# The index key projected ahead of the value tiles, with its narrow columns copied aside

## The chip, the cores and the metric

The kernel runs on one core of a Trainium2 chip, in float32 throughout. The metric is the device time of one execution in microseconds (us); lower is better. Times are medians over several executions, and a profile is of one execution.

## The reference, cut to what matters

The program is two transformer-like blocks over 256 tokens of width 1024. The change lies in the first block, where one normalised and modulated activation `hn` (256 x 1024) is projected by one wide matrix, whose columns are then split:

```
hn   = modulate(rmsnorm(x, norm1_g), shift1, scale1)
proj = hn @ w_in                       # 1024 columns in, 11 groups of columns out
qa, ka, va, qi, ki, wi, qb, kb, vb, ga, gb = split(proj)
score = sum_h relu(qi_h @ ki^T) * wi_h * scale     # index scores choose 64 keys per query
ya = attention over the chosen keys (qa, ka, va, rel_bias)
yb = stick-breaking attention (qb, kb, vb)
mod = silu(c) @ w_ada + b_ada          # six modulation vectors of 1024, used all through the block
```

Three of these groups matter here: the values `va` and `vb` (1024 columns together), the index key `ki` (64 columns) and the index weights `wi` (8 columns, one per index head). The last part of `mod` is computed beside them.

## The kernel before, in words

The kernel is written for the five engines by hand. It is a row of blocks; in each block every engine has its own program, the engines meet through semaphores, and at the end of a block all of them drain and are released together before the next begins.

The activation lies transposed in `k.h` (128 partitions x 8 slices x tokens). Weights stream from HBM through a ring of eight half slots (`k.ring`), four chunks of 1 MB at a time. The order of all chunks is a list made once by `plan()` (line 99), and SyncE issues them in that order: `refill()` (line 185) issues the next load as soon as the chunk that held its place is used up, after waiting for a count of finished tiles that the caller names. `arrived()` (line 201) makes an engine wait for a chunk's landing, `chunk()` (line 208) names its place in the ring.

`opening_inputs()` (line 321) computes the first projections, with tokens along the free axis. `block1_projections()` (line 493) is the stage that the change rewrites:

- TensorE (line 505) computes eight value tiles: four chunks `c` of 256 columns, and for each the two halves `tt` of the tokens, eight products each, into bank `2 * c + tt`. From the fifth chunk it then takes the narrow products of `wi` (8 columns, two halves of tokens x 8 slices, line 517) into bank 1, after VectorE has emptied that bank, and last the index key (line 522) into bank 0, after ScalarE has emptied that. In the program that is 64, 16 and 8 products; the trace shows each of them as two passes, 128, 32 and 16.
- ScalarE (line 527) copies the even banks to `v` and last the index key to `kit` (line 533).
- VectorE (line 536) copies the odd banks to `v` (line 539). Behind each of its four copies stand four or five calls of `ada_column()` (line 294): one column of the modulation each, a product of 1024 elements and a sum (line 305), 18 in this block (4, 5, 4 and 5). After the last it scales the narrow sums into `wi` (line 545) and finishes the modulation (lines 312 and 548).
- GpSimd (line 552) moves the bias rows through HBM and loads further modulation weights, each after a count of finished columns (line 290).

`block1_attention()` (line 572) follows: the index scores on TensorE (line 613), ScalarE (line 711) and VectorE (lines 741, 743), and then sixteen items of attention, with sixteen wide gate tiles (line 639) on TensorE between them. Behind it lie `merge1`, `project_and_square` and the expert layer.

VectorE's and TensorE's order around the end of the stage is set by these lines:

```
for c in range(4):                     # VectorE
    dve.wait_ge(k.tile_ready.sem, k.tile_ready.at(2 * c + 2))
    nc.vector.tensor_copy(v[:, 1, ...], k.bank[2 * c + 1][:, 0:256]).then_inc(k.dve_emptied.sem, 1)
    for j in ...: ada_column(k, dve, j)
```

Of the kernel before, what the change touches and what calls it, by code (L numbers as in the profile page):

```python
# [18 lines left out]
ALU = mybir.AluOpType  # L19
ACT = mybir.ActivationFunctionType  # L20
AX = mybir.AxisListType

P = 128
D = 1024
KD = D // P
TOK = 256
TT = TOK // P
# [5 lines left out]
IDX_SCALE = 64 ** -0.5 * 8 ** -0.5  # L33
# [65 lines left out]
def plan():  # L99

    global NDENSE
    unit = 0
    for name, chunks in (("in1", 10), ("v1", 4), ("ki", 1), ("in1g", 8), ("projab", 4), ("out1", 4), ("wq1", 8), ("keys1", 1), ("wq1", 8), ("keys1", 1),
                         ("uv1", 0), ("in2", 14), ("in2g", 4), ("glu", 1), ("ssmout", 2), ("mlout", 4), ("out2", 4),
                         ("wq2", 8), ("keys2", 1), ("wq2", 8), ("keys2", 1), ("uv2", 0)):
        PHASE[name] = len(LOADS)
        if chunks:
            at = DENSE_AT.setdefault(name, NDENSE)
            for c in range(chunks):
                LOADS.append(("dense", at + c, unit, 2))  # L110
                unit += 2
            NDENSE = max(NDENSE, at + chunks)
            continue
        order = [("u", e) for e in range(NKEYS) if e not in AHEAD_UPS] + [("v", e) for e in range(NKEYS)]
        for side, e in order:
            LOADS.append((side + name[-1], e, unit, 1))
            unit += 1
# [67 lines left out]
def refill(k, sp, n, used, counts, after=None):  # L185


    for c in range(n):
        if after is not None:
            after(c)  # L190
        gone = k.at + c
        for m in range(k.loaded, NLOADS):
            if FREED_BY[m] > gone:
                break
            sig, count = counts[c] if used is None else (used, counts[c])
            sp.wait_ge(sig.sem, sig.at(count))
            load(k, sp, m)
            k.loaded = m + 1


def arrived(k, eng, c):

    n = k.at + c
    slot = LOADS[n][2] % HALVES
    eng.wait_ge(k.w_loaded[slot], ARRIVED[n])


def chunk(k, c):

    _, _, unit, size = LOADS[k.at + c]  # L210
    slot = unit % HALVES
    return k.ring[:, slot:slot + size, :].rearrange("p a n -> p (a n)")
# [96 lines left out]
def ada_finish(k, dve, ch, j0, j1):  # L309

    dve.wait_ge(k.ada_done.sem, k.ada_done.at(j1))
    ch.then(k.nc.vector.tensor_tensor(k.mod[:, j0:j1], k.mod[:, j0:j1], k.vec("b_ada")[:, j0:j1], ALU.add))
# [177 lines left out]
    k.trans_ready.advance(HEADS)  # L490


def block1_projections(k, pt, v, kit, wi, row, bias1):


    nc = k.nc
    with nc.Block() as block:
        @block.sync
        def _(sp):
            refill(k, sp, 5, k.tile_ready, [2, 4, 6, 8, 10])  # L500

        @block.tensor
        def _(pe):
            for c in range(4):
                arrived(k, pe, c)
                w = chunk(k, c).rearrange("p (k n) -> p k n", k=KD)
                for tt in range(TT):
                    for kk in range(KD):
                        ins = nc.tensor.matmul(k.bank[2 * c + tt][:, 0:256], k.h[:, kk, tt * P:(tt + 1) * P], w[:, kk, :],
                                               start=kk == 0, stop=kk == KD - 1)  # L510
                    ins.then_inc(k.tile_ready.sem, 1)
            arrived(k, pe, 4)
            w = chunk(k, 4).rearrange("p (k n) -> p k n", k=KD)
            pe.wait_ge(k.dve_emptied.sem, k.dve_emptied.at(1))
            for tt in range(TT):
                for kk in range(KD):
                    ins = nc.tensor.matmul(k.bank[1][:, tt * 8:tt * 8 + 8], k.h[:, kk, tt * P:(tt + 1) * P],
                                           w[:, kk, P:P + 8], start=kk == 0, stop=kk == KD - 1)
            ins.then_inc(k.tile_ready.sem, 1)
            pe.wait_ge(k.act_emptied.sem, k.act_emptied.at(1))  # L520
            for kk in range(KD):
                ins = nc.tensor.matmul(k.bank[0][:, 0:TOK], w[:, kk, 0:P], k.h[:, kk, 0:TOK],
                                       start=kk == 0, stop=kk == KD - 1)
            ins.then_inc(k.tile_ready.sem, 1)

        @block.scalar
        def _(act):
            for c in range(4):
                act.wait_ge(k.tile_ready.sem, k.tile_ready.at(2 * c + 1))
                nc.scalar.activation(v[:, 0, c * 256:(c + 1) * 256], k.bank[2 * c][:, 0:256], ACT.Copy)\  # L530
                    .then_inc(k.act_emptied.sem, 1)
            act.wait_ge(k.tile_ready.sem, k.tile_ready.at(10))
            nc.scalar.activation(kit[:, :], k.bank[0][:, 0:TOK], ACT.Copy)

        @block.vector
        def _(dve):
            for c in range(4):
                dve.wait_ge(k.tile_ready.sem, k.tile_ready.at(2 * c + 2))
                nc.vector.tensor_copy(v[:, 1, c * 256:(c + 1) * 256], k.bank[2 * c + 1][:, 0:256])\
                    .then_inc(k.dve_emptied.sem, 1)  # L540
                left = ADA_TILES - ADA_IN1
                for j in range(ADA_IN1 + left * c // 4, ADA_IN1 + left * (c + 1) // 4):
                    ada_column(k, dve, j)
            dve.wait_ge(k.tile_ready.sem, k.tile_ready.at(9))
            nc.vector.tensor_scalar(wi[:, :], k.bank[1][:, 0:16], IDX_SCALE, None, ALU.mult)
            ch = Chain(dve, k.dve_step)
            ada_finish(k, dve, ch, ADA_FIRST, ADA_TILES)
            ch.then(nc.vector.scalar_tensor_tensor(k.gain[:, 1, :], k.mod[:, 4 * KD:5 * KD], 1.0, k.vec("norm2_g"),
                                                   ALU.add, ALU.mult))

        @block.gpsimd
        def _(pool):
            def modulation_weights(c):
                pool.wait_ge(k.ada_done.sem, k.ada_done.at(2 * (c - ADA_SLOTS) + 2))
                ada_load(k, pool, c)

            pool.wait_ge(k.bias_rows.sem, k.bias_rows.at(HEADS))
            pool.dma_start(k.bias_dram, row).then_inc(k.bias_dma, 16)
            for c in range(ADA_CALLED, ADA_CALLED + 2):
                modulation_weights(c)  # L560
            pool.wait_ge(k.bias_dma, 16)
            src = bass.AP(k.bias_dram.tensor, P - 1, [[HEADS * 3 * P - 1, P], [3 * P, HEADS], [1, 2 * P]])
            pool.dma_start(bias1[:, :, :], src).then_inc(k.bias_dma, 16)
            for c in range(ADA_CALLED + 2, ADA_TILES // 2):
                modulation_weights(c)
    k.tile_ready.advance(10)
    k.act_emptied.advance(4)
    k.dve_emptied.advance(4)
    k.at += 5


# [1825 lines left out]
def build(nc, args, out, stop=None):  # L2397

    k = K()
# [6 lines left out]
    with ExitStack() as ctx:  # L2406
# [31 lines left out]
        def done(what):  # L2438
            return stop == what
# [16 lines left out]
        with ExitStack() as ctx1:  # L2456
            sb1 = lambda n, s: ctx1.enter_context(nc.sbuf_tensor(n, s, F32))
            pt = sb1("proj_t", [P, 36, TOK])
            v = sb1("values", [P, TT, D])
            kit = sb1("ki_t", [P, TOK])  # L2460
            wi = sb1("wi", [P, 16])
            bias0 = sb1("bias0", [P, HEADS, P])
            bias1 = sb1("bias1", [P, HEADS, 2 * P])
            with ExitStack() as ctx2:
                k.ada = ctx2.enter_context(nc.sbuf_tensor("ada", [P, ADA_SLOTS, 2, D], F32))
                k.cond = ctx2.enter_context(nc.sbuf_tensor("cond", [P, D], F32))
                row = pt[:, 20:32, :].rearrange("p a n -> p (a n)").rearrange("p (h n) -> p h n", h=HEADS)
                opening_inputs(k, vecs, row, bias0[0:BUCKETS, :, :], pt)
                block1_projections(k, pt, v, kit, wi, row, bias1)
            yt = sb1("y_t", [P, KD, TOK])  # L2470
            merged = sb1("merged", [P, KD, TOK])
            block1_attention(k, pt, v, kit, wi, bias0, bias1, yt)
            if done("att"):
                return finish(yt[:, :, :])
            merge1(k, pt, yt, merged)
            project_and_square(k, merged, k.mod[:, 2 * KD:3 * KD], yt, k.choice[:, 0, :])
# [7 lines left out]
        with ExitStack() as ctx1:  # L2484
            sb1 = lambda n, s: ctx1.enter_context(nc.sbuf_tensor(n, s, F32))
# [144 lines left out]
```

## Time and profile before

| | before |
|---|---|
| median of 3 runs | 1990.54 us (1987.36 to 1993.57) |
| profiled execution | 1990.65 us |
| its span in the trace | 1988.8 us |
| TensorE busy | 1923.3 us (97%) |
| VectorE busy | 1265.2 us (64%) |
| ScalarE busy | 471.3 us (24%) |
| GpSimd busy | 349.6 us (18%) |
| mean granted TensorE clock | 0.994 |

The span is the time from the first to the last instruction on the core; 1.85 us of the execution lie around it. Times in the trace count from the span's start. TensorE's busy time is modelled, since its products are pipelined, so 97% does not say that it works at its peak. The granted clock is 1.00 at 2.4 GHz and 0.50 at 1.2 GHz. In the rows, PE is TensorE's products, PEld its weight loads, DVE is VectorE, ACT ScalarE, POOL GpSimd and SP SyncE; a name with q is the engine's sequencer.

### The profile page before, as it was taken

Reading aid. Unit: us, or ns where it says so; the run is one execution under the profiler, and the core shown is the slowest. Engines: PE = TensorE matmul, PEld = TensorE weight load, DVE = VectorE, ACT = ScalarE, POOL = GpSimd, SP = SyncE. Lnnn points to the kernel's source line nnn. Section 1 sums busy time; section 2 is a strip of 40 time slices with the busy share of each in tenths; the row PEclk is TensorE's granted clock in tenths of the full one; section 3 lists DMA queues with packets and bytes.
Section 4 is the critical chain, followed back from the end, with each engine's and each line's share of the span. In section 5 each row is a group of like instructions: output and inputs, shape, how many; then the busy total and the mean of one; then the engine's idle time right before and its main releaser. Section 6 shows DMA issues by size and latency. Waiting matters only on the chain. (4 is left out here: it accounts for less than half of the span.)

```text
span 1988.8 us, 33132 instructions
## 1 busy us (share of the span) xinstructions
PE 1923.3 (97%) x13047; PEld 1803.6 (91%) x13047; DVE 1265.2 (64%) x2827; ACT 471.3 (24%) x1646; POOL 349.6 (18%) x304
## 2 busy tenths in 40 slices
PE   8989999999999999999999989999999999999998
PEld 6877789999999999999988567899999999999998
DVE  6349323899788854444489984219997888544343
ACT  3003302223544410000221024012125444100001
POOL 0100000022332312211000740000223323211110
PEclk9989999999999999999999999999999999999999
DMA  8962238799999999999544130378899999999995
GB/s 308 421 260 100 86 148 346 267 372 331 382 398 390 394 416 413 414 414 413 210 141 157 46 114 1 117 282 323 342 334 370 399 381 398 413 413 414 414 414 213
DMA packets 123356, 604.94 MB, mean 304 GB/s; under 512 B 14589, under 2 KB 16797, under 8 KB 83137
## 3 DMA queue, kind: packets, MB, share of 16 engines
q1 hardware_dynamic: 90832, 379.62, 49.5%
q0 software_dynamic: 30800, 222.07, 27.9%
q8 instruction: 104, 1.70, 0.3%
q10 hardware_dynamic: 1568, 1.12, 0.2%
q14 instruction: 52, 0.42, 0.1%
HBM read 600.14 MB, written 2.62 MB: 303 GB/s over the span
## 5 line engine op out<-in xcount | busy, mean ns | idle before, releaser
L1156 PE MATMUL bank<-expert_coef,ring 128*128 128x160 f32 x4096 | 561.4, 299 | 6.1 <-DVE expert_coef L1490 2.9
L1156 PEld LDWEIGHTS bank<-expert_coef,ring 128*128 128x128 f32 x4096 | 557.0, 190 | 9.8 <-DMA ring<-in_uv 6.2
L1131 PE MATMUL bank<-h,ring 128*128 128x160 f32 x3712 | 521.7, 299 | 0.0
L1131 PEld LDWEIGHTS bank<-h,ring 128*128 128x128 f32 x3712 | 508.1, 190 | 0.0
L1082 POOL DMA_INDIRECT expert_rows<-in_uv,pair_index x192 | 274.3, 1428 | 1273.4 <-DVE pair_sum L1374 504.6
L1367 DVE CUSTOM_DVE_ANT_0 expert_rows<-expert_rows,h_tokens 128x1024 f32<-128x1024 f32 x192 | 234.7, 1222 | 230.9 <-DMA expert_rows<-in_uv,pair_index 230.8
L1374 DVE SCALAR_TENSOR_TENSOR pair_sum<-expert_rows,pair_coef,pair_sum 128x1024 f32<-128x1024 f32 x192 | 246.3, 1283 | 57.2 <-ACT pair_coef L1270 55.7
L1268 ACT ACTIVATE pair_act<-pair_dot 128x1 f32<-128x1 f32 x192 | 38.8, 202 | 520.6 <-DVE pair_dot L1367 520.3
L1097 PE MATMUL bank<-h,ring 128*128 128x128 f32 x1024 | 115.7, 276 | 1.1 <-ACT h L1277 1.1
L1097 PEld LDWEIGHTS bank<-h,ring 128*128 128x128 f32 x1024 | 115.4, 192 | 1.3 <-issue 1.2
L1246 ACT ACTIVATE expert_coef<-bank 128x160 f32<-128x160 f32 (+28 forms) x254 | 65.7, 261 | 157.0 <-PE bank L1131 157.0
L1254 ACT ACTIVATE work<-work,choice 128x128 f32<-128x128 f32 x320 | 102.0, 406 | 0.0
L1481 DVE TENSOR_TENSOR work<-const,choice 128x1024 f32<-128x1024 f32 x80 | 97.4, 1222 | 0.4 <-DVE picked L1473 0.4
L1148 PE MATMUL bank<-work 128*128 128x128 f32 x640 | 84.8, 275 | 5.5 <-ACT work L1254 5.5
L1148 PEld LDWEIGHTS bank<-work 128*128 128x128 f32 x640 | 79.3, 191 | 6.4 <-ACT work L1254 6.4
L1244 ACT ACTIVATE expert_act<-bank 128x4 f32<-128x4 f32 (+24 forms) x150 | 35.9, 239 | 165.9 <-PE bank L1131 164.2
L1490 DVE TENSOR_TENSOR expert_coef<-bank,expert_coef 128x212 f32<-128x212 f32 (+19 forms) x80 | 42.4, 530 | 48.1 <-ACT expert_coef L1262 48.1
L1660 PE MATMUL bank<-h,ring 128*128 128x272 f32 (+1 forms) x320 | 71.9, 387 | 1.0 <-PEq L1056 1.0
L1660 PEld LDWEIGHTS bank<-h,ring 128*128 128x128 f32 x320 | 60.7, 190 | 12.1 <-issue 1.4
L398 PE MATMUL bank<-h,ring 128*128 128x256 f32 x320 | 70.3, 380 | 0.0
L398 PEld LDWEIGHTS bank<-h,ring 128*128 128x128 f32 x320 | 60.4, 190 | 10.2 <-issue 2.2
L1941 POOL TENSOR_TENSOR mixed<-s_z,s_rot 128x256 f32<-128x256 f32 x64 | 49.0, 786 | 100.0 <-DVE s_z L1915 100.0
(389 smaller groups left out, 2040.3 us busy)
## 6 DMA issues: line engine op xcount, KB each, us to landing
ring<-in_uv SPq DMA_DIRECT2D x256, 512.0 KB, 13.5
ring<-in_ut SPq DMA_DIRECT2D x232, 512.0 KB, 7.3
ring<-in_dense SPq DMA_DIRECT2D x96, 1024.0 KB, 5.0
ada<-in_ada POOLq DMA_DIRECT2D x16, 1024.0 KB, 17.6
expert_coef<-in_ut SPq DMA_DIRECT2D x24, 512.0 KB, 9.2
ada<-in_ada SPq DMA_DIRECT2D x8, 1024.0 KB, 24.0
expert_rows<-in_uv,pair_index POOLq DMA_INDIRECT x192, 9.4
bias_rows<-proj_t POOLq DMA_DIRECT2D x1, 1536.0 KB, 6.5
```

What stands on the lines that cost most here:

```text
L398: return nc.tensor.matmul(k.bank[j % BANKS][:, 0:TOK], w[:, kk, (j % 2) * P:(j % 2 + 1) * P], k.h[:, kk, 0:TOK], start=kk == 0, stop=kk == ...
L1082: pool.indirect_dma_start(rows[:, p % BUFFERS, :], None, table, bass.IndirectOffsetOnAxis(pindex[:, p:p + 1], 0))\
L1097: ins = nc.tensor.matmul(k.bank[c % 4][:, 0:P], w[:, kk, (c % 2) * P:(c % 2 + 1) * P], k.h[:, kk, tt * P:(tt + 1) * P], start=kk == 0, sto ...
L1131: ins = nc.tensor.matmul(k.bank[e % 4][:, 0:DENSE], w[:, kk, :], k.h[:, kk, GATHERED:TOK], start=kk == 0, stop=kk == KD - 1)
L1148: ins = nc.tensor.matmul(k.bank[b][:, q * P:(q + 1) * P], second[:, g % BUF, q, :], first[:, g % BUF, q, :], start=True, stop=True)
L1156: ins = nc.tensor.matmul(down_bank(i), w[:, i * P:(i + 1) * P], A[:, e, :], start=e == 0 and i % 3 == 0, stop=e == NB - 1, skip_group_chec ...
L1246: ins = nc.scalar.activation(A[:, e, t:], k.bank[e % 4][:, t:DENSE], gelu)
L1254: ins = nc.scalar.activation(first[:, g % BUF, q, :], first[:, g % BUF, q, :], ACT.Copy, scale=k.choice[:, 2, t:t + 1])
L1367: nc.vector.tensor_tensor_reduce(u, u, htok[:, :], 1.0, 0.0, ALU.mult, ALU.add, dots[:, p:p + 1])\
L1374: nc.vector.scalar_tensor_tensor(acc[:, :], rows[:, p % BUFFERS, D:], pcoef[:, p:p + 1], acc[:, :], ALU.mult, ALU.add).then_inc(k.added.se ...
L1481: nc.vector.tensor_tensor(hots[:, :, g % BUF, :, :], iota.unsqueeze(1).unsqueeze(1).broadcast_to(shape), k.choice[:, 0:2, t:t + GROUP].uns ...
L1660: ins = nc.tensor.matmul(out, left, right, start=kk == 0, stop=kk == KD - 1)
```

## The change

The chunk with the index key and the narrow columns is moved ahead of the four value chunks in the list of loads. TensorE computes the index key first, into bank 7. Meanwhile ScalarE copies the eight narrow columns of that chunk (128 x 8 x 8 elements) into a tile of their own, `wiw`, from which the narrow products then read; TensorE's last product of the index key waits for that copy, and the chunk's place in the ring is given up when the index key is done. The narrow products no longer run in a row: behind each of the first five value tiles stand three of them (six passes), behind the sixth the last one, all into bank 6. The last two value tiles go to banks 6 and 7 and so wait, the seventh for VectorE's fourth release (the scaling of the narrow sums into `wi`), the eighth for ScalarE's first (the copy of the index key). The scaling into `wi` moves in VectorE's program from the end to the place between the third group of columns and the fourth copy. The counts on which SyncE's five loads wait become 1, 3, 5, 7, 10 in place of 2, 4, 6, 8, 10.

```diff
--- before.py
+++ after.py
@@ -100,7 +100,7 @@
 
     global NDENSE
     unit = 0
-    for name, chunks in (("in1", 10), ("v1", 4), ("ki", 1), ("in1g", 8), ("projab", 4), ("out1", 4), ("wq1", 8), ("keys1", 1), ("wq1", 8), ("keys1", 1),
+    for name, chunks in (("in1", 10), ("ki", 1), ("v1", 4), ("in1g", 8), ("projab", 4), ("out1", 4), ("wq1", 8), ("keys1", 1), ("wq1", 8), ("keys1", 1),
                          ("uv1", 0), ("in2", 14), ("in2g", 4), ("glu", 1), ("ssmout", 2), ("mlout", 4), ("out2", 4),
                          ("wq2", 8), ("keys2", 1), ("wq2", 8), ("keys2", 1), ("uv2", 0)):
         PHASE[name] = len(LOADS)
@@ -490,59 +490,68 @@
     k.trans_ready.advance(HEADS)
 
 
-def block1_projections(k, pt, v, kit, wi, row, bias1):
+def block1_projections(k, pt, v, kit, wi, wiw, row, bias1):
 
 
     nc = k.nc
     with nc.Block() as block:
         @block.sync
         def _(sp):
-            refill(k, sp, 5, k.tile_ready, [2, 4, 6, 8, 10])
+            refill(k, sp, 5, k.tile_ready, [1, 3, 5, 7, 10])
 
         @block.tensor
         def _(pe):
+            narrow = [(tt, kk) for tt in range(TT) for kk in range(KD)]
+            arrived(k, pe, 0)
+            w = chunk(k, 0).rearrange("p (k n) -> p k n", k=KD)
+            for kk in range(KD):
+                if kk == KD - 1:
+                    pe.wait_ge(k.recip_ready.sem, k.recip_ready.at(1))
+                ins = nc.tensor.matmul(k.bank[7][:, 0:TOK], w[:, kk, 0:P], k.h[:, kk, 0:TOK],
+                                       start=kk == 0, stop=kk == KD - 1)
+            ins.then_inc(k.tile_ready.sem, 1)
             for c in range(4):
-                arrived(k, pe, c)
-                w = chunk(k, c).rearrange("p (k n) -> p k n", k=KD)
+                arrived(k, pe, 1 + c)
+                w = chunk(k, 1 + c).rearrange("p (k n) -> p k n", k=KD)
                 for tt in range(TT):
+                    if c == 3:
+                        emptied, n = ((k.dve_emptied, 4), (k.act_emptied, 1))[tt]
+                        pe.wait_ge(emptied.sem, emptied.at(n))
                     for kk in range(KD):
                         ins = nc.tensor.matmul(k.bank[2 * c + tt][:, 0:256], k.h[:, kk, tt * P:(tt + 1) * P], w[:, kk, :],
                                                start=kk == 0, stop=kk == KD - 1)
                     ins.then_inc(k.tile_ready.sem, 1)
-            arrived(k, pe, 4)
-            w = chunk(k, 4).rearrange("p (k n) -> p k n", k=KD)
-            pe.wait_ge(k.dve_emptied.sem, k.dve_emptied.at(1))
-            for tt in range(TT):
-                for kk in range(KD):
-                    ins = nc.tensor.matmul(k.bank[1][:, tt * 8:tt * 8 + 8], k.h[:, kk, tt * P:(tt + 1) * P],
-                                           w[:, kk, P:P + 8], start=kk == 0, stop=kk == KD - 1)
-            ins.then_inc(k.tile_ready.sem, 1)
-            pe.wait_ge(k.act_emptied.sem, k.act_emptied.at(1))
-            for kk in range(KD):
-                ins = nc.tensor.matmul(k.bank[0][:, 0:TOK], w[:, kk, 0:P], k.h[:, kk, 0:TOK],
-                                       start=kk == 0, stop=kk == KD - 1)
-            ins.then_inc(k.tile_ready.sem, 1)
+                    for tn, kk in narrow[3 * (2 * c + tt):3 * (2 * c + tt) + 3]:
+                        ins = nc.tensor.matmul(k.bank[6][:, tn * 8:tn * 8 + 8], k.h[:, kk, tn * P:(tn + 1) * P], wiw[:, kk, :],
+                                               start=kk == 0, stop=kk == KD - 1)
+                        if (tn, kk) == narrow[-1]:
+                            ins.then_inc(k.tile_ready.sem, 1)
 
         @block.scalar
         def _(act):
+            arrived(k, act, 0)
+            w = chunk(k, 0).rearrange("p (k n) -> p k n", k=KD)
+            nc.scalar.activation(wiw[:, :, :], w[:, :, P:P + 8], ACT.Copy).then_inc(k.recip_ready.sem, 1)
+            act.wait_ge(k.tile_ready.sem, k.tile_ready.at(1))
+            nc.scalar.activation(kit[:, :], k.bank[7][:, 0:TOK], ACT.Copy).then_inc(k.act_emptied.sem, 1)
             for c in range(4):
-                act.wait_ge(k.tile_ready.sem, k.tile_ready.at(2 * c + 1))
+                act.wait_ge(k.tile_ready.sem, k.tile_ready.at(2 * c + (2 if c < 3 else 3)))
                 nc.scalar.activation(v[:, 0, c * 256:(c + 1) * 256], k.bank[2 * c][:, 0:256], ACT.Copy)\
                     .then_inc(k.act_emptied.sem, 1)
-            act.wait_ge(k.tile_ready.sem, k.tile_ready.at(10))
-            nc.scalar.activation(kit[:, :], k.bank[0][:, 0:TOK], ACT.Copy)
 
         @block.vector
         def _(dve):
             for c in range(4):
-                dve.wait_ge(k.tile_ready.sem, k.tile_ready.at(2 * c + 2))
+                if c == 3:
+                    dve.wait_ge(k.tile_ready.sem, k.tile_ready.at(8))
+                    nc.vector.tensor_scalar(wi[:, :], k.bank[6][:, 0:16], IDX_SCALE, None, ALU.mult)\
+                        .then_inc(k.dve_emptied.sem, 1)
+                dve.wait_ge(k.tile_ready.sem, k.tile_ready.at(2 * c + (3 if c < 3 else 4)))
                 nc.vector.tensor_copy(v[:, 1, c * 256:(c + 1) * 256], k.bank[2 * c + 1][:, 0:256])\
                     .then_inc(k.dve_emptied.sem, 1)
                 left = ADA_TILES - ADA_IN1
                 for j in range(ADA_IN1 + left * c // 4, ADA_IN1 + left * (c + 1) // 4):
                     ada_column(k, dve, j)
-            dve.wait_ge(k.tile_ready.sem, k.tile_ready.at(9))
-            nc.vector.tensor_scalar(wi[:, :], k.bank[1][:, 0:16], IDX_SCALE, None, ALU.mult)
             ch = Chain(dve, k.dve_step)
             ada_finish(k, dve, ch, ADA_FIRST, ADA_TILES)
             ch.then(nc.vector.scalar_tensor_tensor(k.gain[:, 1, :], k.mod[:, 4 * KD:5 * KD], 1.0, k.vec("norm2_g"),
@@ -564,8 +573,9 @@
             for c in range(ADA_CALLED + 2, ADA_TILES // 2):
                 modulation_weights(c)
     k.tile_ready.advance(10)
-    k.act_emptied.advance(4)
-    k.dve_emptied.advance(4)
+    k.act_emptied.advance(5)
+    k.dve_emptied.advance(5)
+    k.recip_ready.advance(1)
     k.at += 5
...
+            wiw = sb1("wi_weights", [P, KD, 8])
...
-                block1_projections(k, pt, v, kit, wi, row, bias1)
+                block1_projections(k, pt, v, kit, wi, wiw, row, bias1)
```

## Rows read from the trace of the kernel before

**Rows 1.** The page, busy time of each engine (share of the span) and instructions.

```profile
PE 1923.3 (97%) x13047; PEld 1803.6 (91%) x13047; DVE 1265.2 (64%) x2827; ACT 471.3 (24%) x1646; POOL 349.6 (18%) x304
```

**Rows 2.** The chain of waits, its earliest piece: start us, us, what.

```profile
1307.91 0.04 issue
```

**Rows 3.** Lines 330 and 497: durations ns min/median/max, first and last start us.

```profile
L330 POOLq DRAIN  x1: 26320/26320/26320, 79.2 to 79.2; - x1
...
L497 POOLq DRAIN  x1: 12738/12738/12738, 118.8 to 118.8; - x1
...
L497 DVEq DRAIN  x1: 19/19/19, 143.3 to 143.3; - x1
```

**Rows 4.** Timeline 135 to 165: start us, us, engine, line, op [idle before <- releaser].

```profile
136.49 0.42 DVE L539 COPY values<-bank 128x256 f32<-128x256 f32 x1 [1.91 <-PE bank L509]
...
140.70 6.12 PE L522 MATMUL bank<-h,ring 128*128 128x256 f32 x16
...
142.56 0.17 DVE L545 TENSOR_SCALAR wi<-bank 128x16 f32<-128x16 f32 x1
...
142.90 0.17 DVE L548 SCALAR_TENSOR_TENSOR gain<-mod,vecs 128x8 f32<-128x8 f32 x1
146.86 0.38 ACT L533 ACTIVATE ki_t<-bank 128x256 f32<-128x256 f32 x1 [13.43 <-PE bank L522]
...
147.62 0.71 PE L613 MATMUL bank<-ki_t,proj_t 64*128 64x128 f32 x8 [0.81 <-PEq L497]
```

**Rows 5.** Waits 147 to 197: us in total, times, longest (first of 18).

```profile
ACT probs_t L686 <- PE bank L650: 23.0, 7, 3.8
```

**Rows 6.** Timeline 105 to 121, the stage's first tiles.

```profile
105.78 6.50 PE L509 MATMUL bank<-ring,h 128*128 128x256 f32 x16 [8.90 <-PEq L330]
...
115.77 0.42 DVE L539 COPY values<-bank 128x256 f32<-128x256 f32 x1 [16.15 <-PE bank L509]
...
120.69 0.09 DVE L305 DVE_READ_ACCUMULATOR2_ANT mod<- 128x1 f32 x1
```

**Rows 7.** Stretches of the stage: us, busy by engine, PEclk, DMA share, GB/s.

```profile
105.78:112.30 6.52, 6.52 (x17) 5.23 (x18) 0.00 (x0) 0.00 (x0) 1.58 (x3) 0.56 0.78 265
112.30:136.45 24.15, 24.15 (x115) 21.26 (x114) 16.15 (x29) 1.54 (x4) 1.98 (x3) 1.00 0.86 342
136.45:140.70 4.25, 4.25 (x33) 4.25 (x32) 4.21 (x8) 0.00 (x0) 0.00 (x0) 0.77 0.69 247
140.70:146.82 6.12, 6.12 (x17) 4.65 (x17) 2.33 (x7) 0.00 (x0) 0.00 (x0) 0.60 0.00 0
147.50:154.80 7.30, 4.82 (x40) 3.05 (x40) 6.04 (x19) 4.63 (x17) 0.00 (x0) 1.00 0.41 147
154.80:196.80 42.00, 42.00 (x230) 33.27 (x228) 39.55 (x115) 15.83 (x53) 0.00 (x0) 1.00 0.29 101
```

**Rows 8.** Stretches around gaps of TensorE, the same columns.

```profile
100.00:102.00 2.00, 0.00 (x0) 0.00 (x0) 0.00 (x0) 0.00 (x0) 0.00 (x0) 0.81 1.01 422
...
109.00:112.30 3.30, 3.30 (x11) 2.66 (x10) 0.00 (x0) 0.00 (x0) 0.00 (x0) 0.63 0.95 285
...
200.00:202.00 2.00, 2.00 (x11) 1.52 (x8) 1.73 (x7) 1.23 (x6) 0.00 (x0) 0.55 0.03 8
...
268.00:270.00 2.00, 0.63 (x3) 0.61 (x4) 0.64 (x2) 0.82 (x1) 0.00 (x0) 1.00 0.78 225
```

**Rows 9.** Timeline at the two shorter gaps of TensorE.

```profile
198.90 0.65 PE L650 MATMUL bank<-const,probs 128*128 128x128 f32 x4 [2.10 <-DVE probs L808]
...
200.70 5.15 PE L639 MATMUL bank<-h,ring 128*128 128x256 f32 x16
...
269.37 2.83 PE L924 MATMUL bank<-merged,ring 128*128 128x256 f32 x12 [2.02 <-PEq L850]
```

**Rows 10.** DMA issues 60 to 170: count, KB each, median us to landing.

```profile
ring<-in_dense SPq DMA_DIRECT2D x12, 1024.0 KB, 8.7
ada<-in_ada POOLq DMA_DIRECT2D x11, 1024.0 KB, 19.1
```

## The prediction, made before the result was known

> **What bounds the kernel now.** The page's head first: TensorE is busy 97% of the span, and the chain of waits runs from 1307.91 us to the end almost wholly through TensorE, but it reaches no further back [rows 1, 2]. So it says nothing on the changed stage, which lies at 105 to 148 us and has to be read by itself. What ties the stage to the end is the closing of its block: every engine drains and is released together. The view of line 497 shows who is late there: POOL's drain is over at 118.8 + 12.7 = 131.5, VectorE's at 143.3 [rows 3]. ScalarE is last, because its copy of the index key (146.86 + 0.38 = 147.24) waits for the last product. The next block's first product starts at 147.62, 0.38 after that copy. VectorE was done at 142.90 + 0.17 = 143.07 and so has 147.24 - 143.07 = 4.17 us to spare [rows 4]. Of the 18 kinds of wait in the 50 us behind the stage none ends on a DMA; the longest is ScalarE's for TensorE [rows 5]. The stage's start (105.78) is set by POOL's drain in the block ahead (79.2 + 26.3 = 105.5), which the change leaves alone [rows 3, 6]. A microsecond at this close is a microsecond at the end, but for what TensorE's clock and the slack in attention give or take, which I bound below.
>
> **TensorE's part.** Each product in the code is two passes in the trace (64 value products, 128 passes). Before, in order:
> - First value tile, 16 passes: 105.78 to 112.28, 6.50 us, at a mean granted clock of 0.56 after the idle gap.
> - Seven value tiles: 112.30 to 136.45, 24.15 us at 1.00, so 3.45 each.
> - 32 narrow passes: 136.45 to 140.70, 4.25 us at 0.77. Weighted by the clock that is 3.27 us at full clock, 0.102 a pass.
> - Index key, 16 passes: 140.70 to 146.82, 6.12 us at 0.60 [rows 6, 7].
>
> After, the index key comes first and pays for the slow start in place of the first value tile: 105.78 + 6.50 = 112.28. Then five value tiles with six narrow passes each, 3.45 + 0.61 = 4.06: the narrow work of the fifth ends at 112.28 + 5 x 4.06 = 132.58. The sixth tile's wide part ends at 136.03, its two narrow passes at 136.24. If nothing held it, TensorE would run two more tiles and be done at 136.24 + 6.90 = 143.14, 3.7 us before the 146.82 of now: 1.0 us from narrow work at full clock, 2.7 us from an index key that no longer follows narrow work at a low clock. (That 22 wide-and-narrow passes keep the clock is supported by attention, 154.8 to 196.8, where 16 wide passes alternate with small ones at 1.00 [rows 7].)
>
> **The new wait.** The last pair of value tiles uses banks 6 and 7. Bank 7 is free when ScalarE has copied the index key at about 112.7. Bank 6 holds the narrow sums, and tile seven waits for VectorE's fourth release, the scaling into wi. In VectorE's program that scaling stands behind the third value copy and its four modulation columns. VectorE does not run it early: in the kernel before, the narrow sums were complete at 140.70 and wi was scaled only at 142.56, behind a column [rows 4].
> VectorE's times after: the first copy can start when the second value tile is done, 112.28 + 4.06 + 3.45 = 119.79; one copy with four columns took 115.77 to 120.78, 5.01 us, so it is free at 124.8 [rows 6]. The second copy starts at 119.79 + 8.12 = 127.91, five columns, about 6.2 us (5.01 and one column more, (5.01 - 0.42) / 4 = 1.15), free at 134.1. The third starts at 136.05, is followed by four columns, and ends at 136.05 + 5.01 = 141.06; wi adds some 0.1, and TensorE gets bank 6 at about 141.2. TensorE has been idle since 136.24: a stall of 5.0 us that the kernel before doesn't have. Queued behind it are the last 32 wide passes, and behind those ScalarE's and VectorE's last copies.
>
> **The clock behind that stall.** No row has an idle gap of 5.0 us. The nearest from above: 8.9 us idle from 96.88, where the clock is 1.00 until 100 and then falls (0.81 over 100 to 102, 0.63 still over 109.0 to 112.3). From below: 2.0 us idle before 269.37, clock 1.00 throughout; and 2.1 us before 198.90, followed by light work, clock 0.55 over 200 to 202 [rows 6, 8, 9]. So a fall is probable, not certain. What it costs: 16 wide passes at a low start took 6.50 and 6.12 in place of 3.45, so 2.7 to 3.05 [rows 7]; the least is 0. I take 2.9. The Trainium skill, page "TensorE: Matmul & The Clock Gate", section "Why this matters for your kernels", speaks against this change: it asks that TensorE be not left idle between bursts of matmuls, because the clock then drops to half, 1.2 of 2.4 GHz. By that rule the sum is the one with 2.9; by the 2.0 us row alone it would be the one with 0, and the 8.9 us row agrees with the page.
> With 2.9, tiles seven and eight run 141.2 + 6.90 + 2.9 = 151.0.
>
> **The tail.** Before, VectorE's last copy, five columns, wi and the finish ran 136.49 to 143.07, 6.58 us, beside the narrow products and the index key; those covered it entirely. After, nothing of TensorE follows the last copy, so the cover is gone. Without wi (0.12) it is 6.46: 151.04 + 6.46 = 157.5. With the 0.38 of the release, the next block's first product starts at 157.9, against 147.62: **+10.3 us**.
>
> **Costed at nothing.** The eight-column copy on ScalarE: it runs while TensorE does seven products of the index key (5.7 us); were that cover gone it would cost 0.2 to 0.4 (the 128x256 copy took 0.38). SP's loads are the same five in the same order of size; the last value chunk is now issued at 112.3, and with 8.7 us to landing it is there 15 us before tile seven could first ask for it [rows 10]; uncovered it would cost those 8.7. POOL's last modulation load waits for a column that comes some 4 us later (122.9 in place of 118.8), and so the drain ends near 136, 21 us before VectorE; the load (19.1 us to landing) is there by 142, ahead of the last two columns at about 154.
>
> **Behind the stage.** TensorE will have been idle from 151.0 to 157.9, so attention starts at a low clock where it now has 1.00. The index part has 4.82 us of TensorE in 7.30 [rows 7]; doubled, it passes the stretch by at most 2.3 us. The first wide tile behind it can lose 3.05. Against that, TensorE waits 2.10 us for VectorE at 198.90, and the clock fall at 200 us, where 16 wide passes took 5.15 against a value tile's 3.45, can go away: up to 1.7 gained [rows 9]. So -1.7 to +5.4; nearest to the middle is that the slack at 198.9 takes most of it: I take +0.7.
> Sum: 10.3 + 0.7 = **+11.0 us**. The profiled execution took 1990.65 us (span 1988.8 and 1.85 around it), 0.1 above the median of 1990.54, so I use it: 1990.65 + 11.0 = **2001.7 us**.
>
> **Rivals.**
> 1. The clock holds over the stall (the 2.0 us row for it, the 8.9 us row against). Tiles seven and eight end at 148.1, VectorE at 154.6, next block 155.0: +7.4, and attention starts as now: 1998.0. Chance 17%.
> 2. The stall doesn't bind, only the tail does (wi reaches TensorE before the columns). For it: nothing but the wait's being on another signal than I read. TensorE ends at 143.14, VectorE at 149.6, release 150.0: +2.4, 1993.0. Chance 8%.
> 3. Faster: the tail doesn't bind either. Its place is VectorE after 143.14; it decides if VectorE's rest there were under 4.1 us, so that the close comes before 147.62. Then TensorE's end and a copy set the close, 143.14 + 0.42 + 0.38 = 143.9: -3.7, 1987.0. Against it: five columns of 1.15 us stand behind the last copy. Chance 5%.
> 4. The change doesn't do what it says: spread by threes the narrow passes still bring the clock down, as 32 in a row do from 136.45 on [rows 7]. If it halved for the five mixed tiles, they would take 17 to 20 us more and the time would be near 2020. Attention's mixture at 1.00 is against it. Chance 4%.
>
> **How the numbers follow.** The forecast has 66%. Its own range, with -1.7 to +5.4 behind the stage, is 1999.2 to 2006.3. Rival 1 with the lowest of those bounds is 1996.3; taking that in and leaving the highest corner and rivals 2 to 4 out gives 1996.0 to 2005.5. This kernel can tell 0.3%, about 6 us, from no change. Slower by more than that: 66 + 4 and 15 of rival 1, 85%. Within it: rival 2 and 2 of rival 1, 10%. Faster: 5%.
>
> **What would show it.** TensorE's first value tile starting at 112.3; narrow passes in sixes at clock 1.00 to 136; a TensorE gap near 136.2 to 141.2 that ends on VectorE's wi; the tile behind it at a low clock; VectorE's columns running alone for 6 us behind TensorE's last product; the block's close set by VectorE's drain near 157.5. I am wrong if TensorE's gap is missing, if the close still falls on ScalarE, or if attention makes up more than 4 us.

## The result, and the profile after

The changed kernel took 2013.13 us in the median of four executions (2003.57, 2004.61, 2021.65 and 2022.88), the kernel before 1989.3 in the same comparison: a ratio of 1.0115, 95% interval 1.0079 to 1.015. The forecast was 2001.7, 1996.0 to 2005.5. The executions come in two groups some 18 us apart, and the median of four lies between them; that gap is what the experiments had to explain. The profiled execution is one of the lower group: 2003.57 us, span 2001.8 against 1988.8.

First the changed stage. Timeline of the changed kernel, TensorE and VectorE with one line of ScalarE, from the stage's start to the next block's first product (start us, us, engine, line, operation [idle before <- releaser]); these lines answer to [rows 4, 6]:

```profile
105.32 6.67 PE L510 MATMUL bank<-h,ring 128*128 128x256 f32 x16 [8.49 <-PEq L330]
111.83 3.62 PE L521 MATMUL bank<-ring,h 128*128 128x256 f32 x16
...
115.28 0.73 PE L525 MATMUL bank<-wi_weights,h 128*128 128x8 f32 x6
...
119.40 0.73 PE L525 MATMUL bank<-wi_weights,h 128*128 128x8 f32 x6
...
135.90 0.28 PE L525 MATMUL bank<-wi_weights,h 128*128 128x8 f32 x2
136.10 0.43 DVE L550 COPY values<-bank 128x256 f32<-128x256 f32 x1 [2.10 <-PE bank L521]
...
141.02 0.17 DVE L547 TENSOR_SCALAR wi<-bank 128x16 f32<-128x16 f32 x1
...
141.33 9.19 PE L521 MATMUL bank<-ring,h 128*128 128x256 f32 x32 [5.15 <-DVE wi L547]
147.11 0.38 ACT L539 ACTIVATE values<-bank 128x256 f32<-128x256 f32 x1 [14.75 <-PE bank L521]
150.56 0.43 DVE L550 COPY values<-bank 128x256 f32<-128x256 f32 x1 [9.38 <-PE bank L521]
...
156.97 0.17 DVE L557 SCALAR_TENSOR_TENSOR gain<-mod,vecs 128x8 f32<-128x8 f32 x1
...
157.69 6.21 PE L623 MATMUL bank<-ki_t,proj_t 64*128 64x128 f32 x32 [7.17 <-PEq L497]
```

TensorE's gap is there, 5.15 us, and it ends on VectorE's wi. The last copy and its five columns run alone from 150.56 to 157.14. The next block starts at 157.69, 10.07 us after the kernel before. From the stage's first product to the next block's first the changed kernel takes 51.8 to 52.4 us in its five profiles, and the old stage 41.8 and 41.9 in the two profiles that have it unaltered (before and e6_before_held): 9.9 to 10.5 us more. The stage's own start lies at 104.5 to 107.3 us in the five, so a single time in one profile against one in another is good to a microsecond or two.

The same stage by stretches (busy time of PE, PEld, DVE, ACT, POOL, then the granted clock), which answers to [rows 7]:

```profile
105.30:111.85 6.55, 6.53 (x17) 5.27 (x18) 0.00 (x0) 0.26 (x1) 1.59 (x3) 0.54 0.77 264
111.85:136.15 24.30, 24.30 (x129) 21.76 (x127) 11.21 (x21) 1.54 (x4) 1.99 (x3) 1.00 0.84 340
136.15:141.30 5.15, 0.03 (x1) 0.00 (x0) 5.04 (x10) 0.00 (x0) 0.00 (x0) 0.74 0.55 204
141.30:150.52 9.22, 9.19 (x32) 7.47 (x32) 0.00 (x0) 0.38 (x1) 0.00 (x0) 0.77 0.00 0
150.52:157.66 7.14, 0.01 (x1) 0.00 (x0) 6.50 (x13) 0.00 (x0) 0.00 (x0) 0.86 0.41 147
157.66:165.27 7.61, 6.56 (x40) 4.45 (x40) 6.06 (x19) 4.85 (x17) 0.00 (x0) 0.68 0.01 3
165.27:207.00 41.73, 41.73 (x230) 33.27 (x228) 39.30 (x115) 15.56 (x53) 0.00 (x0) 1.00 0.29 101
```

The mixed tiles keep the clock at 1.00. It falls in the gap (0.74) and is low under tiles seven and eight (0.77, 9.2 us; at 1.00 the same two tiles take 7.1, as two experiments below show). It falls again while the columns run alone (0.86) and is low under the index part of attention (0.68), which takes 7.6 us in place of 7.2. The close of the block, line 497, against [rows 3]: VectorE's drain is now the last. In the kernel before ScalarE's was (from 146.9 us on, 0.40 us); now that ended some ten microseconds earlier.

```profile
L497 ACTq DRAIN  x1: 414/414/414, 147.1 to 147.1; - x1
...
L497 DVEq DRAIN  x1: 19/19/19, 157.4 to 157.4; - x1
```

Attention's first gate tile starts at 165.27 against 154.83 (+10.4). 1034 us later the projections of the mLSTM, a part of block 2, start at 1199.0 against 1188.6: still +10.4. The other 2.6 of the 13.0 us are in block 2, which the change doesn't touch. Stretches of the kernel before, then of the changed one, each from the gap ahead of the projections to the end of the mLSTM's heads, the work that follows the projections:

```profile
1185.00:1188.50 3.50, 0.00 (x0) 0.00 (x0) 3.28 (x9) 0.00 (x0) 0.00 (x0) 1.00 0.73 243
1188.50:1212.40 23.90, 22.51 (x144) 16.85 (x144) 10.19 (x24) 9.62 (x19) 7.23 (x8) 1.00 0.02 9
1212.40:1246.20 33.80, 32.25 (x181) 25.20 (x180) 17.67 (x64) 14.47 (x44) 0.87 (x2) 1.00 0.00 1
```

```profile
1195.50:1199.00 3.50, 0.00 (x0) 0.02 (x1) 3.21 (x9) 0.00 (x0) 0.00 (x0) 1.00 0.78 257
1199.00:1224.50 25.50, 24.18 (x144) 17.93 (x144) 10.18 (x24) 9.61 (x19) 7.25 (x8) 0.93 0.02 6
1224.50:1259.80 35.30, 33.81 (x182) 26.64 (x181) 17.70 (x64) 14.49 (x44) 0.87 (x2) 0.95 0.00 1
```

The work is the same (144 and some 180 passes); the clock fell once in each stretch, at 1200 and at 1231, and each fall cost about 1.5 us. Of these 3.1 us some 0.5 is made up again further on.

### The profile page after: what moved, and what is told of

It reads as the page before. It is cut to its first block and busy times, and to the rows that moved or that the text cites. A ratio compares the mean times of both kernels' runs of the same rounds, so it can differ in the third digit from the quotient of the medians.

```text
span 2001.8 us, 33133 instructions
## 1 busy us (share of the span) xinstructions
PE 1926.6 (96%) x13047; PEld 1806.3 (90%) x13047; DVE 1265.4 (63%) x2827; ACT 472.2 (24%) x1647; POOL 350.7 (18%) x304
## 5 line engine op out<-in xcount | busy, mean ns | idle before, releaser
L1377 DVE CUSTOM_DVE_ANT_0 expert_rows<-expert_rows,h_tokens 128x1024 f32<-128x1024 f32 x192 | 234.7, 1222 | 232.0 <-DMA expert_rows<-in_uv,pair_index 231.9
```

The costliest lines, as they stand in the source:

```text
L1377: nc.vector.tensor_tensor_reduce(u, u, htok[:, :], 1.0, 0.0, ALU.mult, ALU.add, dots[:, p:p + 1])\
```

## The experiments

**The changed kernel again**, unaltered, four times.

> The changed kernel, unaltered. Its one profile so far shows +10.4 us at the first tile of attention's gates and +10.4 still at 1199 us, then +13.0 at the end, where TensorE's clock falls twice in block 2 (1200 and 1230 us); two other executions took 18 us more at a mean clock of 0.979. Theory A (the stage gives +10.4 each time; the rest is TensorE's clock falling in block 2, in some executions for longer): executions come in groups, the lowest near +13, others near +30, and the mean clock tells them apart; in a profile of a slow one the stage still reads +10.4. Theory B (the stage itself is worse in the slow executions, a stall of some 28 us in place of 5): a slow profile shows the close of the stage near 175 us.

> The changed kernel once more, unaltered, for more executions. Of nine so far two lay near 2022 and seven at 2001 to 2005. If it is chance per execution, none to two of these lie near 2020 and the rest at 2001 to 2005; if the first chip or session made it, none does.

> The changed kernel, unaltered, for the odds of its slow executions: 3 of 18 so far, against 2 of 53 of the kernel before. If the odds are the same for both (about 5 of 71), these runs and e11_after_fourth bring one or none in ten; if the change raises them, two or more.

> As e10_after_third: the changed kernel, unaltered. Fast executions at 2001 to 2006, slow ones near 2022.

Measured: medians 2002.53, 2002.41, 2005.31 and 2002.57, ratios 1.0064 (1.0048 to 1.0079), 1.0059 (1.0027 to 1.009), 1.0058 (1.0028 to 1.0087) and 1.0041 (1.0015 to 1.0067). With the first four that makes 42 executions: 38 at 1999.9 to 2009.8, and 4 at 2021.3 to 2022.9, these at a mean clock of 0.979 or 0.980. The kernel before, in the comparisons beside all runs, has 87 (one of 2897 us, at a mean clock of 0.651, is left out): 81 at 1986.6 to 1996.6 and 6 at 2007.5 to 2012.0, at 0.981 to 0.983. So one execution in ten of the one and one in fifteen of the other is some 18 us longer: these odds can't be told apart, so nothing shows that the change makes the longer executions more frequent. Over all of them the medians are 2003.6 and 1991.6, 12.0 apart. No profile of the changed kernel fell into an execution near 2022, so theory B of e1_after, that its stage itself is worse there, is not answered by a profile of its own. The profile of e11_after_fourth (1999.89 us, span 1998.1, 9.3 over the profile of before) shows the stage as above, started 1.3 us earlier than before's, and no fall in block 2: there the projections start at 1197.46 and the heads take what they took before. The five profiles of the changed kernel show 0, 0, 1, 2 and 2 such falls, in executions of 1999.89, 2001.26, 2002.40, 2003.57 and 2006.38 us. The unaltered kernel before has one profile, with none, so whether the change makes these short falls more frequent isn't shown.

**The wait alone: wi ahead of the columns.**

```diff
-                if c == 3:
-                    ...                # the same wait and scaling, ahead of the fourth copy
                 dve.wait_ge(k.tile_ready.sem, ...)
                 nc.vector.tensor_copy(v[:, 1, ...], ...).then_inc(k.dve_emptied.sem, 1)
+                if c == 2:
+                    dve.wait_ge(k.tile_ready.sem, k.tile_ready.at(8))
+                    nc.vector.tensor_scalar(wi[:, :], k.bank[6][:, 0:16], IDX_SCALE, None, ALU.mult)...
                 for j in ...: ada_column(k, dve, j)
```

> The changed kernel with the scaling into wi put directly behind the third value copy, ahead of that group's four columns. Theory A: TensorE's gap before tile seven shrinks from 5.2 to about 0.6 us, the clock stays at 1.00, its last tile ends at 143.6 in place of 150.5; VectorE's copy, five columns and finish still follow alone, 143.6 + 6.5, so the next block starts at 150.4, +2.8 us against 147.6 of the kernel before. Were the tail no limit it would start at 144.4, -3.2. The total: 2.8 us over the kernel before, plus what block 2's clock falls cost, 0 to 18.

Measured in the stage, timeline:

```profile
111.26 3.62 PE L521 MATMUL bank<-ring,h 128*128 128x256 f32 x16
...
136.18 7.14 PE L521 MATMUL bank<-ring,h 128*128 128x256 f32 x32 [0.57 <-DVE wi L550]
...
143.36 0.42 DVE L546 COPY values<-bank 128x256 f32<-128x256 f32 x1 [2.75 <-PE bank L521]
...
149.77 0.17 DVE L557 SCALAR_TENSOR_TENSOR gain<-mod,vecs 128x8 f32<-128x8 f32 x1
...
150.49 6.73 PE L623 MATMUL bank<-ki_t,proj_t 64*128 64x128 f32 x32 [7.17 <-PEq L497]
```

A gap of 0.57 us, two tiles in 7.1, the tail unchanged, the next block at 150.49: +2.9, where +2.8 was expected. The next block starts 7.2 us earlier than in the changed kernel. Of that 6.6 are the edit's: 4.6 of gap (5.15 less 0.57) and 2.0 of clock (9.19 less 7.14); the other 0.6 comes from a shorter slow start at the head of the stage (second tile at 111.26 in place of 111.83). The twelve executions lie in three groups: six at 1994.5 to 1997.7, three at 2003.8 to 2004.2, three at 2013.6 to 2015.7 (ratio 1.005, 1.0024 to 1.0077). No profile shows the middle group. The profile fell into the highest, 2013.64 us, and so shows where such an execution loses its time. Its stretches in block 2, beside those above:

```profile
1187.20:1190.80 3.60, 0.00 (x0) 0.02 (x1) 3.31 (x9) 0.00 (x0) 0.00 (x0) 1.00 0.69 239
1190.80:1216.40 25.60, 24.28 (x145) 17.92 (x145) 10.28 (x24) 9.69 (x20) 7.25 (x8) 0.93 0.02 8
1216.40:1269.50 53.10, 52.21 (x180) 39.92 (x179) 17.77 (x64) 14.42 (x43) 0.87 (x2) 0.58 0.00 0
```

The heads take 53.1 us in place of 33.8: 19.3 us, as much as the 18 to 19 between the lowest and the highest group. The clock falls at 1222, six us into that stretch, and doesn't come back until 1266.5, when it is nearly over.

**The shift alone**: the kernel before, with twenty scalings of 128x1024 on VectorE at the end of the stage.

```diff
+            for _ in range(20):
+                ch.then(nc.vector.tensor_scalar(k.cond[:, :], k.cond[:, :], 1.0, None, ALU.mult))
```

> The kernel before with twenty scalings of a tile that is no longer read (128x1024 each) at the end of VectorE's program in the changed stage, some 14.4 us, so that the stage closes near 157.9 as in the changed kernel, with none of the change's edits. Theory A (what comes in block 2 is caused by the shift in time alone): the same falls of the clock in block 2 and executions at +13 and at +30. Theory C (they come from something in the new code: its banks, its instructions, its order): a flat +10.4 from the stage to the end, all executions within 4 us of each other.

> e3_delay once more (the kernel before with 14.5 us of VectorE work at the end of the stage): five executions at 2001 to 2007 so far, none near 2020. If the shift in time raises the odds of the slow block, one in six of these is near 2020; if they come with the new code, none.

Measured: the next block starts at 157.68, as in the changed kernel (157.69). 17 executions, 2000.4 to 2010.5, median 2004.3, ratios 1.0065 (1.0048 to 1.0083) and 1.0042 (1.0012 to 1.0073); none near 2020. A delay of this stage with none of the new code costs what the change costs. The profiles show falls in block 2 here too (1198 and 1229 in the first, 1203 and 1233 in the second). So for the short falls theory C, that they come with the new code, is out. On the executions near 2020 the 17 don't decide. None is what theory C expects and against the shift in time; but at 4 in 42, the changed kernel's own rate, none in 17 has a chance of some 18%. What speaks against theory C there is that the kernel before has executions some 18 us longer of its own, 6 in 87.

**The clock in the gap alone**: the changed kernel with eleven unread products in the gap.

```diff
                 for tt in range(TT):
+                    if c == 3 and tt == 0:
+                        pe.wait_ge(k.act_emptied.sem, k.act_emptied.at(1))
+                        keep_busy(k, 11, k.bank[7][:, 0:TOK], k.h[:, 0, 0:TOK])
                     if c == 3:
```

> The changed kernel with eleven products that no one reads (256 columns, into bank 7) ahead of tile seven's wait, so that TensorE isn't idle in the 5.2 us gap; the wait itself stays. It tells the stall from its clock. Theory A: the clock stays at 1.00, tiles seven and eight take 6.9 us in place of 9.2, and the next block starts at 155.2 to 155.6 in place of 157.7: some 2.3 us less than the changed kernel, 7.7 over the kernel before at that place. Rival: the clock falls anyway or the added products end late; then no less than 157.7.

Measured, stretches of the gap and of the two tiles behind it, then timeline:

```profile
136.00:141.10 5.10, 4.89 (x24) 3.97 (x23) 4.48 (x9) 0.00 (x0) 0.00 (x0) 1.00 0.60 206
141.10:148.10 7.00, 6.61 (x31) 5.49 (x29) 0.35 (x2) 0.38 (x1) 0.00 (x0) 1.00 0.00 0
```

```profile
140.54 7.17 PE L524 MATMUL bank<-ring,h 128*128 128x256 f32 x32 [0.21 <-DVE wi L550]
154.88 5.46 PE L626 MATMUL bank<-ki_t,proj_t 64*128 64x128 f32 x26 [7.17 <-PEq L497]
```

The clock stays at 1.00, the tiles take 7.2 us, and the block starts at 154.88, 2.8 us earlier than in the changed kernel (0.8 of that is its earlier tile: 140.54 against 141.33). So the fall behind the gap is worth some 2 us (9.19 less 7.17). Twelve executions, median 2000.95, ratio 1.0037 (1.0008 to 1.0066).

**The tail taken away**: wi early, and ten of the 18 columns ahead of the first copy.

```diff
+            for j in range(ADA_IN1, ADA_IN1 + 10):
+                ada_column(k, dve, j)
             for c in range(4):
...
-                for j in range(ADA_IN1 + left * c // 4, ADA_IN1 + left * (c + 1) // 4):
+                for j in range(ADA_IN1 + 10 + (0, 4, 6, 8)[c], ADA_IN1 + 10 + (4, 6, 8, 8)[c]):
                     ada_column(k, dve, j)
```

> As e2_wi_early, and ten of VectorE's 18 modulation columns ahead of its first copy, where it has been idle for 14 us, then four, two and two behind the first three copies and none behind the last. Theory A: nothing is left behind TensorE's last tile but a copy and the finish, so the next block starts at 143.6 + 0.42 + 0.4 + 0.4 = 144.8, 2.8 us ahead of the kernel before; 1987 us if block 2 keeps its clock, up to 18 more if the shift brings it down. Rival: the columns wait for their weights (the loads of the last four land after 124 us) and TensorE waits for bank 6 again; then the next block starts at 148 or later.

Measured in the stage:

```profile
111.11 3.62 PE L521 MATMUL bank<-ring,h 128*128 128x256 f32 x16
...
143.22 0.42 DVE L548 COPY values<-bank 128x256 f32<-128x256 f32 x1 [5.04 <-PE bank L521]
...
143.78 0.17 DVE L558 SCALAR_TENSOR_TENSOR gain<-mod,vecs 128x8 f32<-128x8 f32 x1
...
144.50 0.72 PE L624 MATMUL bank<-ki_t,proj_t 64*128 64x128 f32 x8 [1.32 <-PEq L497]
```

The next block starts 3.1 us earlier than before, but 1.3 of that is a shorter slow start, which isn't the edit's (the first 16 passes took 5.2 us here and 6.5 before and in the changed kernel). From the second tile's first product, where the clock is at 1.00, to the next block's first it is 35.3 us before, 45.9 in the changed kernel, 39.2 with wi early and 33.4 here. So the wait with its clock is worth 6.6 us and the uncovered tail 5.8, and with both gone the stage is 1.9 us shorter than before: 6.6 + 5.8 - 1.9 = 10.5. In the total it can't be told from no change: twelve executions, median 1989.31 against 1991.11, ratio 1.0009 (0.9988 to 1.003). Two of the twelve lie at 2006; the profiled one is 2.9 us below the profile of before.

**Holding the clock in block 2**: five unread products around the four small ones that open the heads, in the changed kernel, the kernel before, and the one just told.

```diff
+            keep_busy(k, 1, k.bank[7][:, 0:TOK], k.const[:, 0:TOK])
             for h in range(MH):
                 ins = nc.tensor.matmul(k.bank[h // 2][...], sel[:, h, :], rows[:, 5, META:], ...)
...
+                keep_busy(k, 1, k.bank[7][:, 0:TOK], k.const[:, 0:TOK])
```

> The changed kernel with five more busy-work products (256 columns, no one reads them) at the start of the last mLSTM block, one ahead of and one behind each of its four small products of four rows. Theory A (executions near 2014 to 2022 are those in which TensorE's clock falls at that place and stays low through the block, 53.2 us in place of 33.7): all executions lie within 5 us, at 2001 to 2006, none near 2020, and the block takes 34 to 36 us. Theory D (the clock comes down for a reason ahead of the block, or what makes some executions slow is not in it): some executions still lie 9 or 18 us above the others.

> The same five products in the kernel before. Theory A: 1987 to 1994 with at most 2 us added, none near 2007; e5_after_held lies 10.4 to 13 us above it, which is the change's own price without the lottery in block 2. Theory D: as likely as before to have an execution near 2007, and a distance to e5_after_held that differs from 10.4 to 13.

> e4_cols_early (wi early, ten columns ahead of the first copy) with the same five products. Theory A: 3 us below e6_before_held, near 1986 to 1988, none near 2006. Theory E (the 3.1 us that the stage gains are given back in attention, where VectorE and TensorE run close to each other): within 1 us of e6_before_held.

Measured: 2008.84 (six executions, 2007.4 to 2010.3), 1996.19 (twelve, 1991.5 to 2000.4) and 1995.1 (twelve, 1989.2 to 1998.1); ratios to the kernel before 1.0085 (1.0072 to 1.0098), 1.0022 (1.0012 to 1.0033) and 1.0014 (1.0003 to 1.0025). None of the 30 lies apart from its group; at the 16 in 182 of all kernels without these products some 2.6 would have, so that alone is a hint and no proof. The cost was forecast at 2 us at most and is 3.9 in the kernel before and some 6 in the changed one: the fall still comes, but the clock is back after 3.5 us. Stretches of e5_after_held:

```profile
1232.00:1234.00 2.00, 2.00 (x7) 1.00 (x8) 0.83 (x5) 1.67 (x6) 0.00 (x0) 1.00 0.00 0
1234.00:1236.00 2.00, 2.00 (x6) 1.59 (x5) 2.00 (x10) 1.73 (x6) 0.00 (x0) 0.50 0.00 0
1236.00:1238.00 2.00, 2.00 (x7) 1.62 (x7) 0.40 (x3) 0.18 (x1) 0.00 (x0) 0.65 0.02 4
1238.00:1240.00 2.00, 2.00 (x15) 1.89 (x14) 0.49 (x3) 0.00 (x0) 0.00 (x0) 1.00 0.00 0
```

With no execution far from its group, the change costs 2008.84 - 1996.19 = 12.65 us between these medians, inside the 10.4 to 13 expected. The products themselves cost the changed kernel some 2 us more than the kernel before, and 12.65 holds that too; their two profiled executions lie 9.8 apart (spans 2005.6 and 1995.8). The median of e7_cols_held lies 1.1 below that of e6_before_held, between the 3 of theory A and theory E's 1 or less. Their profiles speak against theory E: e7_cols_held is 2.2 us ahead at the next block's start (145.90 against 148.08), 3.3 ahead at the projections of block 2 (1186.38 against 1189.65) and 3.5 at the end. The two medians stand over spreads of 9 us, so 1.1 and 3 aren't clearly told apart.

## Why the prediction was right or wrong

- **The new wait.** Gap of 5.0 forecast, 5.15 measured, ended by wi. Right; e2_wi_early takes it away.
- **The clock behind it.** 2.9 forecast (bounds 0 to 3.05); 9.19 less the 7.14 and 7.17 of e2_wi_early and e9_stall_busy is 2.0. Right that it falls, 0.9 too high. Rival 1 is out.
- **The tail.** 6.46 forecast; the copy to the finish took 150.56 to 157.14, 6.58, and e4_cols_early gets 5.8 back. Right. Its release takes 0.55 us, not 0.38. Rivals 2 and 3 are out.
- **The mixed tiles.** 4.06 each forecast; from one tile's narrow passes to the next 115.28 to 119.40, 4.12, at clock 1.00. Rival 4 is out.
- **The stage.** +10.3 forecast, +10.07 measured. The two tiles behind the gap were 0.6 us shorter than forecast; gap, tail and release together made up most of it.
- **Behind the stage.** +0.7 forecast, in bounds of -1.7 to +5.4 that I drew from attention alone. Attention gave +0.4. Its index part had 1.7 us more of TensorE (6.56 in place of 4.82), of which 0.4 showed; the rest went into time in which TensorE had waited before. The clock was back at 1.00 before the first wide tile. The slack at 198.9 took nothing: the same wait of 2.10 us stands at 209.35, and the clock falls behind it as it did at 200.
- **The step that failed.** It isn't in attention. It is this one: "A microsecond at this close is a microsecond at the end, but for what TensorE's clock and the slack in attention give or take, which I bound below." The sum has no term for block 2. I looked for changes of the clock in the 50 us behind the stage and took the rest of the span as fixed, because the one profile of before shows the clock at 1.00 through the mLSTM part of block 2. It is one execution. In the changed kernel's five profiles that part loses 0, 0, some 1.5, 3.1 and some 3 us to falls of the clock, and in the profile of e2_wi_early about 21, 19.3 of them in the heads. By their time and mean clock alone, 4 in 42 executions of the changed kernel and 6 in 87 of the kernel before are of the long kind. Two of the first four were, which is chance as far as the 38 later ones show, with two among them; their median of 2013 holds half of it. With all 42 the median is 2003.6, inside the range that was forecast.

So the mechanism of the changed stage holds, and the price of the change comes out near the forecast: 12.0 us between the medians of 42 and 87 executions, 12.65 between those with the five products, against 11.0. What was missing is the term for block 2 and, for a median of so few executions, its odds: +2.6 us in the profiled execution, some +18 in two of four.

Shown by a profile is that an execution near 2014 of e2_wi_early loses its 19 us in the heads. For the changed kernel's own executions near 2022 it is inferred: their distance and mean clock fit (a mean clock of 0.979 in place of 0.991 over 2020 us is 48 us more at half clock; e2_wi_early's is low from 1222 to 1266.5), but no profile fell into one, and none into an execution of the kernel before near 2010. What decides which execution gets the long fall stays open.

## What to carry to other kernels

A release given in program order costs what stands ahead of it on its engine, and work that was hidden behind another engine's last products is uncovered when these are moved ahead: read both from the engine's own queue, not from the idle engine. Here two such terms, 6.6 and 5.8 us, stood against 1.9 us of stage saved. Giving the release ahead of the columns, and moving ten of these into VectorE's idle time before the first copy, turned the stage from +10 to about -2, though in the whole time that can't be told from no change. Before a change of some 10 us is judged, look at the spread of the same kernel: a median of four that lies between two groups says little.

## What the runs showed of the hardware

- TensorE's clock doesn't fall at a fixed time behind the same work. Ahead of the changed stage, in the kernel before, the last product ended at 96.9 us, and the clock was 1.00 up to 100 and 0.81 over 100 to 102; in e11_after_fourth it ended at 96.2, and the clock was 0.50 from 100 on; in e2_wi_early it ended at 97.6, and the clock was 1.00 up to 102.
- The stage's gap of 5.15 us brought the clock down in all five profiles of the changed kernel (tiles seven and eight took 9.1 to 10.1 us). The gap of 3.6 us ahead of block 2's projections did so in 11 of the 14 profiles: the first 32 passes behind it then take 9.26 us, and in before, e1_after and e11_after_fourth, where the clock stays at 1.00, 7.57. The clock can fall behind such a gap with the next products already running: in the changed kernel it was 1.00 up to 1200, the products ran from 1199.0 on, and it was low over 1200 to 1203.5. The lines of before and of the changed kernel:

```profile
1188.59 7.57 PE L2108 MATMUL bank<-s_rot 128*128 128x272 f32 x32 [3.65 <-PEq L2003]
...
1199.01 9.26 PE L2118 MATMUL bank<-s_rot 128*128 128x272 f32 x32 [3.64 <-PEq L2013]
```

- The clock can stay low for long under work that keeps TensorE busy. The stretch of the heads takes 33.8 us at 1.00; in e2_wi_early it took 53.1 at a mean of 0.58, with TensorE busy 52.2 of them. Ten wide passes ahead of the heads ran in every kernel: in the changed kernel's profile the clock came back during them (fall at 1231, back at 1234), in that of e2_wi_early it didn't (fall at 1222, back at 1266.5). The Trainium skill, page "TensorE: Matmul & The Clock Gate", section "HAM oscillation — how this bites in real kernels", tells of throughput lost each time that waits between products bring the clock down. Here it was one fall, which lasted 44 us.
